# A two-block transformer kernel: where squares are summed, how the last chain's gates run, and where the first rotations stand

## The reference, cut to what matters

```
def rms_norm_2(x, g):
    y = x * lax.rsqrt(jnp.mean(x * x, axis=-1, keepdims=True) + EPS)
    return y * g

x = x + gt1 * rms_norm(mix_out, norm_mix_post[l])   # a post-norm
h = rms_norm(x, norm_ffn_pre[l]) * (1.0 + sc2) + sh2 # the pre-norm behind it
```

## Time and profile before

| | |
|---|---|
| runs | 3818.44, 3816.6, 3817.96 us; median 3817.96 |
| profiled execution | 3810.04 us, span 3808.3 us |
| mean granted clock of PE | 0.951 |
| PE busy | 3475.8 us (91%), 20608 matmuls |
| DVE busy | 2042.4 us (54%) |
| ACT busy | 1053.1 us (28%) |
| POOL busy | 1663.6 us (44%) |

### The profile page before, as it was taken

One profiled execution on the slowest core, in us unless ns is written; L12 is line 12 of the kernel. 1 busy time (PEld: TensorE's weight loads), 2 busy tenths in 40 slices (PEclk: granted clock), 3 DMA queues, 4 the chain that ended last, 5 costly groups with the idle time before them and its releaser, 6 DMA issues.

```text
span 3808.3 us, 55665 instructions
## 1 busy us (share of the span) xinstructions
PE 3475.8 (91%) x20608; PEld 2780.2 (73%) x20608; DVE 2042.4 (54%) x3169; ACT 1053.1 (28%) x1960; POOL 1663.6 (44%) x1323
## 2 busy tenths in 40 slices
PE   5998999999699969998899899988999889999998
PEld 3666777777588857776577788877778577778886
DVE  3347777765556553422716575655440644566656
ACT  2142322222111113532416221112551324331112
POOL 2413222225376743143242566655226142466665
PEclk8999999999899989899899999998999999999999
DMA  4341111112233312021021233322103011123232
GB/s 176 114 146 51 40 35 33 36 35 67 81 100 94 98 56 66 23 71 52 24 71 34 77 94 94 97 80 78 34 28 92 26 61 40 58 81 94 96 98 89
DMA packets 71672, 268.48 MB, mean 71 GB/s; under 512 B 7841, under 2 KB 7969, under 8 KB 68385
## 3 DMA queue, kind: packets, MB, share of 16 engines
q1 hardware_dynamic: 67968, 257.98, 21.5%
q10 hardware_dynamic: 3488, 7.51, 0.6%
HBM read 263.37 MB, written 2.10 MB: 70 GB/s over the span
## 4 chain that ended last, share of the span: by engine, by line
PE 74%; DVE 18%; issue 3%; ACT 3%; DMA 1%; DVEq 0%; POOL 0%; ACTq 0%; POOLq 0%
PE psum_a L555 11%; PE psum_a L559 11%; PE psum_a L558 11%; PE psum_d L616 4%; PE psum_d L555 4%; PE psum_d L559 4%; PE psum_d L558 4%; PE psum_d L711 3%; PE psum_a L667 3%; PE psum_d L1006 2%; PE psum_d L636 2%; PE psum_a L581 1%; PE psum_a L584 1%; PE psum_a L585 1%; DVE arena L1967 1%
## 5 line engine op out<-in xcount | busy, mean ns | idle before, releaser
L2882 POOL TENSOR_TENSOR w_lo<-raw,w_hi 128x1024 fp32r<-128x1024 f32 x440 | 1107.5, 2517 | 36.8
L2878 POOL TENSOR_TENSOR mark<-mark 128x1 f32<-128x1 f32 x438 | 104.2, 238 | 2070.4 <-PE psum_a L555 1581.0
L555 PE MATMUL psum_a<-h_hi,w_hi 128*128 128x512 f32 x1936 | 777.3, 402 | 5.2 <-ACT arena L1842 5.2
L558 PE MATMUL psum_a<-h_lo,w_hi 128*128 128x512 f32 x1936 | 765.5, 395 | 0.0
L559 PE MATMUL psum_a<-h_hi,w_lo 128*128 128x512 f32 x1936 | 765.1, 395 | 0.0
L2879 POOL TENSOR_SCALAR w_hi<-raw 128x1024 fp32r<-128x1024 f32 x440 | 468.5, 1065 | 31.9 <-DMA raw<-in_weights 31.9
L555 PEld LDWEIGHTS psum_a<-h_hi,w_hi 128*128 128x128 f32 x1936 | 372.4, 192 | 90.2 <-issue 6.8
L558 PEld LDWEIGHTS psum_a<-h_lo,w_hi 128*128 128x128 f32 x1936 | 372.2, 192 | 77.4 <-issue 1.2
L559 PEld LDWEIGHTS psum_a<-h_hi,w_lo 128*128 128x128 f32 x1936 | 370.6, 191 | 79.5
L555 PE MATMUL psum_d<-split,w_hi 128*128 128x512 f32 x848 | 331.2, 391 | 10.3 <-DVE x L2646 6.7
L559 PE MATMUL psum_d<-split,w_lo 128*128 128x512 f32 x848 | 330.1, 389 | 0.0
(11 more groups left out here) (355 smaller groups left out, 5493.6 us busy)
## 6 DMA issues: line engine op xcount, KB each, us to landing
raw<-in_weights SPq DMA_DIRECT2D x440, 512.0 KB, 3.6
plain<-in_ada SPq DMA_DIRECT2D x20, 1024.0 KB, 7.1
arena<-in_ada SPq DMA_DIRECT2D x4, 1024.0 KB, 10.4
x<-in_x ACTq DMA_DIRECT2D x2, 2048.0 KB, 19.8
out<-x SPq DMA_DIRECT2D x8, 256.0 KB, 3.5
arena<-in_pe ACTq DMA_DIRECT2D x2, 512.0 KB, 3.5
const<-in_const ACTq DMA_DIRECT2D x1, 836.0 KB, 32.0
arena<-in_masks ACTq DMA_DIRECT2D x1, 640.0 KB, 26.9
```

Source lines behind the costliest of these rows:

```text
L555: m = pe.eng.matmul(dst, wh, hi(t), start=t == 0, stop=False)
L558: pe.eng.matmul(dst, wh, lo(t), start=False, stop=False)
L2878: eng.tensor_tensor(b.mark[:, 1:2], b.mark[:, 0:1], b.mark[:, 0:1], ALU.add)
L2882: eng.tensor_tensor(lo, b.raw[:, s], hi.bitcast(F32), ALU.subtract).then_inc(sig["w_ready"], 1)
```

## The change

**Squares.** `dve_sums` is cut into `dve_sum`, one addition. In seven norms (`summed=True`) DVE's program makes addition n-1 right behind the eviction of tile n (or behind the gated addition of tile n), and the last one behind the last eviction. In the first norm of layer 1 ACT squares tile n-1 right behind the sigmoid of gate n.

**Sums on PE.** The pre-norm on x behind each of the two post-norms (of the first block's feed-forward part, and of layer 0) has no DVE additions. PE multiplies each squared tile with the ones, four matmuls a tile, adding up in four psum banks.

**Gates of the last chain.** The four gate products go to ring "d", half before `second` and half behind it. DVE copies them out, and ACT takes the sigmoid in place.

**Rotations.** Rotation n-4 stands behind product n, for n from 4 to 11; the last four stand behind the last product.

```
+def pe_norm_direct(pe, N):
+    b, tiles = pe.b, [pe.tile("a") for _ in range(NQ)]
+    pe.eng.wait_ge(tiles[-1].free, pe.emptied(tiles[-1]))
+    for t in range(KD):
+        pe.eng.wait_ge(pe.sem["sq_direct"], pe.due("sq_direct"))
+        for q, tl in enumerate(tiles):
+            m = pe.eng.matmul(tl.ps[:, 0:1], N.sq[:, t % 2, q * P:(q + 1) * P], b.ones[:, 0:1], start=t == 0, stop=t == KD - 1)
...
+def act_norm_direct(a, N, src, width, dst, bias=None):
...
+    for t in range(KD):
+        a.eng.wait_ge(a.sem["x_ready"], a.due("x_ready"))
+        if t >= 2:
+            a.eng.wait_ge(a.sem["sq_read"], base + t - 1)
+        a.eng.wait_ge(a.sem[a.last], a.own())
+        a.eng.activation(N.sq[:, t % 2], src(t), ACT.Square).then_inc(a.sem["sq_direct"], a.up("sq_direct"))
...
+def dve_sum(v, N, k, t):
+    v.eng.wait_ge(v.sem["sq"], v.due("sq"))
+    name = "sum_ready" if t == k - 1 else "sq_used"
+    if t:
+        v.eng.wait_ge(v.sem[v.last], v.own())
+        v.eng.tensor_tensor(N.acc, N.sq[:, 0] if t == 1 else N.acc, N.sq[:, t % 2], ALU.add)\
+            .then_inc(v.sem[name], v.up(name))
...
@@ eviction of the out product's tiles (four more places alike)
         v.eng.tensor_copy(b.Y8[:, n], v.bank()).then_inc(v.sem["free_d"], v.up("free_d"))
         v.eng.wait_ge(v.sem[v.last], v.own())
         v.eng.sem_inc(v.sem["y_ready"], v.up("y_ready"))
+        if n:
+            dve_sum(v, b.N1, KD, n - 1)
+    dve_sum(v, b.N1, KD, KD - 1)
...
@@ PE, last chain
         chain.first(c)
-        pe_features(pe, "a", "gate", H)
+        tl = pe.tile("d")
+        pe.eng.wait_ge(tl.free, pe.emptied(tl))
+        pe_product(pe, tl.ps, "gate", *H, KD, None, part=range(0, 4))
         chain.second(c)
+        pe_product(pe, tl.ps, "gate", *H, KD, None, part=range(4, KD)).then_inc(tl.full, pe.up("full_d"))
         chain.third(c)
...
@@ DVE, last chain, ahead of dve_rwkv_state
+        v.eng.tensor_copy(b.G_SG[3 + c], v.bank()).then_inc(v.sem["free_d"], v.up("free_d"))
...
@@ ACT, layer 0's gates
+        if square and n:
+            square(n - 1)
...
@@ PE, rotations
+    for n in range(4, 12):
+        raws.append(pe_features(pe, "a", "qk", H))
+        rotate(n - 4)
+    for n in range(8, 12):
+        rotate(n)
```

More of the change, by code:

```diff
@@ L647, in pe_norm @@
     pe_spread(pe, pe.b.col[:, 188:192], 1, P)
+def pe_norm_direct(pe, N):
[5 more added lines that the diff above has]
+            m = pe.eng.matmul(tl.ps[:, 0:1], N.sq[:, t % 2, q * P:(q + 1) * P], b.ones[:, 0:1], start=t == 0, stop=t == KD - 1)
+            if t == KD - 1:
+                m.then_inc(tl.full, pe.up("full_a"))
+            elif q == NQ - 1:
+                m.then_inc(pe.sem["sq_read"], pe.up("sq_read"))
+    pe.eng.wait_ge(pe.sem["norm_inv"], pe.due("norm_inv"))
+    tl = pe.tile("d")
+    pe.eng.wait_ge(tl.free, pe.emptied(tl))
+    for q in range(NQ):
+        at = 188 + tiles[q].n % BANKS
+        m = pe.eng.matmul(tl.ps[:, q * P:(q + 1) * P], b.col[:, at:at + 1].to_broadcast([P, P]), b.ident,
+                          start=True, stop=True)
+    m.then_inc(tl.full, pe.up("full_d"))
 def pe_norm_sums(pe, N):
@@ L1529, in act_rwkv_tail @@
         act_rwkv_chunk(a, W)
-        act_late_gate(a, 3 + c)
         act_rwkv_chunk(a, U)
         act_rwkv_chunk(a, Y[c])
+        a.eng.wait_ge(a.sem["plain_gate"], a.due("plain_gate"))
+        a.eng.wait_ge(a.sem[a.last], a.own())
+        a.eng.activation(b.G_SG[3 + c], b.G_SG[3 + c], ACT.Sigmoid).then_inc(a.sem["late_gate"], a.up("late_gate"))
         if c < NQ - 1:
@@ L1946, in each, with dve_norm @@
         return mask.unsqueeze(1).to_broadcast([P, n, mask.shape[1]])
-def dve_norm(v, N, k, between=None):
-    dve_sums(v, N, k)
+def dve_norm(v, N, k, between=None, summed=False):
+    if not summed:
+        dve_sums(v, N, k)
     dve_inverse(v)
@@ L1955, in dve_norm @@
     return dve_spread(v)
+def dve_sum(v, N, k, t):
[5 more added lines that the diff above has]
+            .then_inc(v.sem[name], v.up(name))
 def dve_sums(v, N, k):
     for t in range(k):
[L1961 to L1968, removed]
+        dve_sum(v, N, k, t)
 def dve_inverse(v):
@@ L1986, in dve_spread_used, with dve_norm_split @@
     v.eng.sem_inc(v.sem["free_d"], v.up("free_d"))
-def dve_norm_split(v, N, k, src, gain, hi, lo, bias=None, between=None):
-    inv = dve_norm(v, N, k, between)
+def dve_norm_split(v, N, k, src, gain, hi, lo, bias=None, between=None, summed=False):
+    inv = dve_norm(v, N, k, between, summed)
     for t in range(k + 1):
@@ L2742, in dve_program @@
         dve_rwkv(v, j)
-    for c in range(NQ - 1):
+    for c in range(NQ):
+        v.eng.wait_ge(v.sem["full_d"], v.due("full_d"))
+        v.eng.wait_ge(v.sem[v.last], v.own())
+        v.eng.tensor_copy(b.G_SG[3 + c], v.bank()).then_inc(v.sem["free_d"], v.up("free_d"))
+        v.eng.wait_ge(v.sem[v.last], v.own())
+        v.eng.sem_inc(v.sem["plain_gate"], v.up("plain_gate"))
+        if c == NQ - 1:
+            break
         dve_rwkv_state(v, KD - 1, c)
```

85 lines of the change are left out of this document (62 added, 23 removed).

## The result

The changed kernel took 3772.65 us (median of 4 runs, 3769.32 to 3775.72) beside 3817.28 us for the kernel before on the same chip: ratio 0.9883, 95% interval 0.9866 to 0.990. That is 44.6 us less, where 42.7 had been summed, and 3775 forecast. On another occasion it took 3776.24 us beside 3817.23 (41.0 us less by the medians, 37.8 by the means), ratio 0.9905, interval 0.9888 to 0.9923. The two intervals, 38 to 51 us and 29 to 43 us, share the range from 38 to 43; a closer figure isn't to be had from times.

The account below looks back on a forecast made before the run. PE (TensorE) sets the end, its longest waits being for DVE's additions in the norms. Seven terms sum to 42.7 us off the profiled 3810.04, giving 3767.3, or 3775 as a median; range 3764 to 3789 us.

Parts of the forecast that it names:

- Rotations, 6.8: First attention: eight rotations behind a product each no longer wait for DVE; gain 6.8 us, bounds 4.4 to 7.6.
- 12 x 0.885 = 10.6 us: First attention: PE's own time for twelve rotations; with 0.1 us for each of eight returns to products, 11.4 us.
- Post-norm sums, 9.2: Norms after out and down products: PE's sum starts 1.9 us after the last eviction, not 6.47; gain 4.6 us each.
- Direct sums, 8.2: Norms on x after both post-norms: PE sums squared tiles at half clock and sets the pace; gain 4.1 us each.
- The rival that they run at the full clock: Direct sums at full clock (+4.6 us), part of "The clock helps more": gain 50 us, 3768 us, chance 0.22.
- Feed-forward norms, 10.0: Both layers: 4.0 us less pause plus 1.0 us of clock, gain 5.0 us each; bounds 4.0 and 6.5.
- Last norms, 5.4: Last norm of both layers: PE starts at 2550.8, not 2553.50; gain 2.7 us each, together bounds 2 and 9.2.
- at 0.69 us and some 0.05 between them: 5.2 us: Last norms: DVE's time for three evictions and four additions after addition 3, which POOL's instruction delays.
- Layer 1's first norm, 2.7: Nine DVE operations left at 0.75 us, so PE starts at 2612.6, not 2615.33; gain 2.7 us, bounds 0 and 4.6.
- Last chain, 0.4: Gates in halves fill PE's waits but DVE's copies cost time; net gain 0.4 us, bounds 1.6 gained, 0.5 lost.
- that wait already exists once, 0.66 us: Last chain: PE's next chunk waits for DVE's state update; there DVE comes late and the 0.69 us copy is paid in full.
- a stretch that stays within 1 us: Sign named for the last chain: its span in the trace stays within 1 us.

Follow-up runs that it names:

- u_h: Changed kernel with only layer 1's first norm put back, its squares and sums behind the gates again; 3780.11 us, ratio 0.9903 to the kernel before.

## Why the prediction was right, term by term

The result lies in the forecast's range, and most waits went the way that was stepped through. The terms were less exact than their sum.

**Rotations, 6.8.** The mechanism was right: no rotation waits for DVE. Mis-sized: from 18.2 us the pass went to seven times 0.91 (the pitch by which the changed kernel's blocks come later, return to the product included) and 3.89 for the last five in a row, 10.2 us. That is a gain of 8.0, above the upper bound of 7.6. The step is "12 x 0.885 = 10.6 us" with 0.1 for each return: 0.885 is a sixth of a run whose length holds the end of its last record, and five in a row took 0.78 each. The stages as wholes, 7.1 and 7.4, hold up to 2.7 us of scatter.

**Post-norm sums, 9.2.** Right: 4.1 and 5.4 when undone. The first sum stands 2.49 us behind the last product, where 2.6 had been named, and 2.48 at the second place; the pauses were 7.20 and 7.13, so 9.4 together.

**Direct sums, 8.2.** The mechanism was right in each step: 0.215 us per record at 0.50, PE as the pace, the end 3.9 us behind the last x tile (4 had been named). The two stages as wholes gave 17.4 us, which is the sum of their terms (8.7 each). Undone alone the direct sums gave 6.5 or 9.0 by the two profiles, 7.5 in the medians. Read in place, from DVE's first multiplication to the sum's end, it is 20.30 less 16.07, 4.2 us in each norm: 8.5. The rival that they run at the full clock didn't come: here the clock was 0.50 from before their first record to behind their last, and with fillers it fell to 0.50 among them. The Trainium skill, TensorE: Matmul & The Clock Gate (Part 1), says that sustained matmul activity releases the throttle. In this case's traces the clock stayed at 1.00 for 23 us where dense fillers stood between bf16 sums; through 13.78 us of fp32 sums without a gap it did not rise, and with two fillers per tile between fp32 sums it fell, with PE as busy (9.05 of 9.20 us) as where it stayed (22.30 of 23.00).

**Feed-forward norms, 10.0.** Right: the pauses went from 6.20 to 2.21 and from 6.14 to 2.16 us, 4.0 each as stepped through, and the stages by 4.7 and 5.3, so the clock gave 0.7 and 1.3 where 1.0 was counted.

**Last norms, 5.4.** Mis-sized: 1.7 us each, the pauses are 5.4 and not 4.4 us. The step that failed is the seven operations "at 0.69 us and some 0.05 between them: 5.2 us". Between an eviction and an addition DVE's queue takes 0.21 us, where a signal and a wait for ScalarE stand, and 0.10 between an addition and the next eviction. At 0.85 us the seven take 5.9; and POOL's instruction is 2.71 us long in the changed kernel, not 2.40. Over the whole trace of the changed kernel it took 2.65 to 2.74 us in all 128 cases in which DVE was in an operation on two SBUF inputs as it began, and 2.34 to 2.40 in all 107 with no DVE instruction beside it. Layer 0's gain isn't read from the stage, which moves by 1.6 without any change, but from its pause, 7.13 to 5.38.

**Layer 1's first norm, 2.7.** It gave 1.1. The pause ahead of the sum went from 9.44 to 6.97, 2.5 us, 1.5 of it by the order of squares and sums (u_h), the other 1.0 along with the squares that no longer stand behind the wait at the end of the gates; 0.6 of that is read directly. The step that failed was left out of the prediction: that PE's start is all that changes. The root's table load, 1.28 us, had run beside the wait for the sum and now follows it, which takes 1.3 us back at the spread.

**Last chain, 0.4.** It cost 0.9, beyond the bound of 0.5 lost. The 1.6 us of waits went nearly as named, to 0.2. The step that failed is "that wait already exists once, 0.66 us": with the copy in front of the state update PE waits ahead of each of the three next chunks, 2.8 us in all where it was 0.7, so all three copies are paid in full. Both kernels without the copies are 0.9 us shorter from block 60 to 64. The prediction's sign for it, a stretch that stays within 1 us, came true, but could not tell this loss from the gain.

**The sum.** Read in place the gains are 8.0 + 9.4 + 8.5 + 10.0 + 3.5 + 1.1 - 0.9 = 39.6 us. The 42.7 of the prediction is near that partly by luck: rotations, first sums and direct sums had been put 1.7 us too low together, last norms, layer 1's first and the last chain 4.8 us too high. By times the gain was 44.6 and 41.0. The difference of 8 us between the profiled execution and the median, carried over unchanged, was not a property of the kernel: executions of either kernel differ by that much through where the clock is low.

## What to carry to other kernels

Sums that stand behind the last eviction can be laid beside the earlier ones at nearly their full worth if the engine idles between evictions; where it alternates without a pause, price each pair by a pair's pitch in the trace, with the signal and the wait between them. Look at what stood under the old wait as well: a table load of 1.28 us that had been hidden there came out at one norm and took back half of the gain. When TensorE reduces tiles itself, price the pass by its records at the clock that holds there, and try a narrower type if the result allows it: bf16 squares gave back 6.5 to 9 us of stage time in two norms. A pause of TensorE costs again behind it, through the clock: dense matmuls on old data in the pauses of two norms alone were worth 6.4 us of stage time. And compare no two profiles of such kernels before one kernel has been profiled twice: here one kernel's stages differed by up to 2.7 us.

## What the runs showed of the hardware

- The clock can fall under a TensorE that is all but always busy: at 1007.7 us after 9.05 busy us of 9.20, with eight one-column fp32 records and two dense matmuls per tile. In another kernel it stayed at 0.50 for 26.7 us in which PE worked for 25.0, about half of that on dense matmuls.
- With dense work right behind a product stream and hardly a gap (22.30 busy us of 23.00) the clock stayed at 1.00 through a double norm. A sum of eight records then takes 1.05 instead of 1.87 us, and the products behind begin at the full clock.
- The same program took 3773.7 and 3767.9 us between first and last instruction, at mean clocks 0.953 and 0.955: 2 x 0.002 x 3770 = 15 us less at half clock, half of which is lost time, 8 us with clocks rounded so, against 5.8 measured.
- Four bf16 one-column matmuls take 0.25 to 0.27 us, the fp32 ones (eight records) 1.05 us at the full clock and 1.70 at half: a quarter or less, not the half that the count of records gives.
- POOL's 128x1024 subtraction lasts 2.4 us alone and 2.7 us when DVE is in an operation on two SBUF inputs as it begins; the DVE addition that it catches ends some 0.56 us behind it.
